# A fourth body for experts of at most 64 rows: the down projection with two products in place of three

## The reference

```
logits = h @ w_router + b_router                     # 256 x 8
top_logit, top_idx = top_k(logits, 2)
top_w = softmax(top_logit)
out_e = (silu(xb @ w1[e]) * (xb @ w3[e])) @ w2[e]    # w1, w3: 1024 x 3584, w2: 3584 x 1024
y = sum of top_w * out_e over the two experts of a token
```

## Time and profile before

| | us |
|---|---|
| median of 3 runs | 1878.74 (1877.62 to 1879.38) |
| the profiled execution | 1881.26 |
| its span, first to last instruction | 1879.6 |
| PE busy | 1727.6 (92%) |
| DVE busy | 1422.7 (76%) |
| ACT busy | 1042.6 (55%) |
| DMA | 502.62 MB, mean 267 GB/s |

### The profile page before, as it was taken

One profiled execution on the slowest core, in us unless ns is written; L12 is line 12 of the kernel. 1 busy time (PEld: TensorE's weight loads), 2 busy tenths in 40 slices (PEclk: granted clock), 3 DMA queues, 4 the chain that ended last, 5 costly groups with the idle time before them and its releaser, 6 DMA issues.

```text
span 1879.6 us, 22711 instructions
## 1 busy us (share of the span) xinstructions
PE 1727.6 (92%) x7882; PEld 1384.3 (74%) x7883; DVE 1422.7 (76%) x1201; ACT 1042.6 (55%) x817; POOL 25.6 (1%) x31
## 2 busy tenths in 40 slices
PE   1899979997999958999999989999999899999995
PEld 0687758886787736878878878888788787887884
DVE  7786877766686874897888875556589688888887
ACT  1464434433364424776767755545577676776773
POOL 0100000000100000000000000000000000000000
PEclk9898989999998977999999999999999999999998
DMA  9874458765474353998998975666599799899991
GB/s 359 308 278 157 157 179 302 280 224 180 170 284 156 112 202 113 361 364 311 366 340 304 378 277 178 211 231 210 192 371 370 256 372 365 301 368 335 340 368 66
DMA packets 210563, 502.62 MB, mean 267 GB/s; under 512 B 9137, under 2 KB 13409, under 8 KB 210481
## 3 DMA queue, kind: packets, MB, share of 16 engines
q1 hardware_dynamic: 208770, 496.15, 73.9%
q0 software_dynamic: 1712, 5.43, 0.9%
HBM read 500.50 MB, written 1.05 MB: 267 GB/s over the span
## 4 chain that ended last, share of the span: by engine, by line
PE 84%; DVE 8%; issue 5%; ACT 1%; DMA 1%; DVEq 0%; POOL 0%; ACTq 0%; SPq 0%; POOLq 0%
PE ps L1343 24%; PE ps L1344 23%; PE ps L1345 23%; PE ps L1349 2%; PE ps L1350 2%; PE ps L1737 2%; PE ps L1850 2%; DVE mod_acc L853 1%; PE ps L1778 1%; DVE stats L873 1%; PE ps L1467 1%; DVE w_lo L1224 1%; DVE w_lo L828 1%; DVE gates L1022 1%; DVE hbuf L890 1%
## 5 line engine op out<-in xcount | busy, mean ns | idle before, releaser
L1224 DVE TENSOR_TENSOR w_lo<-w_raw,w_hi 128x2048 fp32r<-128x2048 f32 x333 | 762.2, 2291 | 224.7 <-ACT w_hi L716 216.9
L716 ACT CAST w_hi<-w_raw 128x2048 fp32r<-128x2048 f32 x333 | 635.4, 1910 | 240.9 <-PE ps L1345 177.1
L1343 PE MATMUL ps<-w_hi,actT_hi 128*128 128x512 f32 (+1 forms) x1536 | 611.7, 398 | 22.6 <-issue 9.9
L1345 PE MATMUL ps<-w_hi,actT_lo 128*128 128x512 f32 (+1 forms) x1536 | 598.6, 390 | 0.0
L1344 PE MATMUL ps<-w_lo,actT_hi 128*128 128x512 f32 (+1 forms) x1536 | 598.0, 389 | 0.0
L1343 PEld LDWEIGHTS ps<-w_hi,actT_hi 128*128 128x128 f32 x1536 | 293.1, 191 | 89.6 <-issue 24.8
L1345 PEld LDWEIGHTS ps<-w_hi,actT_lo 128*128 128x128 f32 x1536 | 292.4, 190 | 60.9
L1344 PEld LDWEIGHTS ps<-w_lo,actT_hi 128*128 128x128 f32 x1536 | 293.1, 191 | 58.8 <-issue 2.3
L828 DVE TENSOR_TENSOR w_lo<-w_raw,w_hi 128x2048 fp32r<-128x2048 f32 x90 | 205.8, 2288 | 120.1 <-ACT w_hi L464 119.7
L464 ACT CAST w_hi<-w_raw 128x2048 fp32r<-128x2048 f32 x90 | 171.3, 1908 | 131.3 <-PE ps L1345 116.8
L1343 PE MATMUL ps<-w_hi,gT_hi 128*128 128x512 f32 x536 | 218.2, 407 | 16.9 <-DVE gT_lo L1247 13.1
(11 more groups left out here) (234 smaller groups left out, 1132.3 us busy)
## 6 DMA issues: line engine op xcount, KB each, us to landing
w_raw<-in_exp_w_dram SPq DMA_DIRECT2D x336, 1024.0 KB, 5.8
w_raw<-in_ffn_w_dram SPq DMA_DIRECT2D x33, 1024.0 KB, 5.2
w_raw<-in_w_mod_mix_dram SPq DMA_DIRECT2D x24, 1024.0 KB, 9.4
w_raw<-in_w_mod_ffn_dram SPq DMA_DIRECT2D x24, 1024.0 KB, 5.7
w_raw<-in_w_gate_dram SPq DMA_DIRECT2D x24, 1024.0 KB, 5.6
w_raw<-in_w_in_dram SPq DMA_DIRECT2D x14, 1024.0 KB, 7.5
w_raw<-in_w_out_dram SPq DMA_DIRECT2D x8, 1024.0 KB, 5.0
w_raw<-in_w_branch_c_dram SPq DMA_DIRECT2D x4, 1024.0 KB, 5.0
```

What stands on the lines that cost most here:

```text
L716: nc.scalar.copy(w_hi[:, i % SPLIT, :], w_raw[:, i % RING, :]).then_inc(split_hi, 1)
L1224: TTn(w_lo[:, i % SPLIT, :], w_raw[:, i % RING, :], w_hi[:, i % SPLIT, :].bitcast(F32), ALU.subtract).then_inc(piece_used, 1)
L1343: MM(to, hi, w_h, start=first, stop=False)
L1345: return MM(to, lo, w_h, start=False, stop=last)
```

## The change

A fourth body, `expert(1, few=True)`, takes experts of at most 64 rows. It packs high and low part for the down projection alone; the up projections stay as in `expert(1)`. Its `gT_hi` copy and its low part have 64 columns per 128 (128x256 in place of 128x512), the low part goes to columns 64 to 127 of the same tile, and `place` gets its second copy of 64 rows. `second_block` is gone from all three engines; the gather of a second block now stands at the start of the bodies for more than 128 rows, and one-block bodies only raise its semaphores.

```diff
ACT
-                    gathered_rows(0, 1)
-                    second_block(0, 1)
+                    gathered_rows(0, 1)
                     with nc.Fori(0, EXPERTS, ...) as e:
-                        def expert(blocks, packed=False):
+                        def expert(blocks, packed=False, few=False):
 gT_part:
-                                    n = HALF_P if b and packed else P
+                                    n = HALF_P if few or b and packed else P
 places:
-                                if packed:
+                                if packed or few:
+                                    half = blocks - 1
                                     ins.then_inc(place_copied, 1)
                                     act.wait_ge(place_copied, e + 1)
-                                    ins = A(place[HALF_P:P, 1, :], ps[0:HALF_P, 0, SEQ:2 * SEQ], ACT.Copy)
+                                    ins = A(place[HALF_P:P, half, :], ps[0:HALF_P, 0, half * SEQ:(half + 1) * SEQ], ACT.Copy)
 body's start:
+                            if blocks == 2:
+                                gathered_rows(1, e + 1)
+                            else:
+                                act.sem_inc(xg_hi_ready[1], 1)
 tail:
                                     gathered_rows(0, e + 2)
-                                    second_block(e + 1, e + 2)
DVE (its gathered_rows and second_block change in the same way)
 gT_part:
-                                for b in range(whole):
+                                for b in range(0 if few else whole):
                                     ins = TTn(gT_lo[:, b, :, :], ...)
-                                if packed:
-                                    ins = TTn(gT_hi[:, 1, :, HALF_P:P], ...)
+                                if packed or few:
+                                    half = blocks - 1
+                                    ins = TTn(gT_hi[:, half, :, HALF_P:P], ...)
PE
 body's start:
+                            pe.wait_ge(xg_hi_ready[0], e + 1)
+                            pe.wait_ge(xg_lo_ready[0], e + 1)
+                            if blocks == 2:
+                                gather(1, e + 1)
+                                pe.wait_ge(xg_hi_ready[1], e + 1)
+                                pe.wait_ge(xg_lo_ready[1], e + 1)
+                            else:
+                                pe.sem_inc(gathered_hi[1], 1)
+                                pe.sem_inc(gathered_lo[1], 1)
 down:
-                                            ins = multiply(b)(bank(2 * b + n), ...)
+                                            ins = (packed_product if few else multiply(b))(bank(2 * b + n), ...)
 end:
                                 gather(0, e + 2)
                                 scatter()
-                                second_block(e + 1, e + 2)
all three, at the choice of the body:
                         with pe.Else():
-                            expert(1)
+                            with pe.If(count > HALF_P):
+                                expert(1)
+                            with pe.Else():
+                                expert(1, few=True)
```

More of the change, by code:

```diff
@@ L814, in _ @@
                         with act.Else():
-                            expert(1)
+                            with act.If(count > HALF_P):
+                                expert(1)
+                            with act.Else():
+                                expert(1, few=True)
                     for t in range(TT):
@@ L1309, in tail @@
                                         TTn(part, part, bank(2 * t + c), ALU.add).then_inc(added, 1)
-                                if not last:
-                                    second_block(e + 1, e + 2)
                             with dve.If(e < EXPERTS - 1):
@@ L1323, in _ @@
                         with dve.Else():
-                            expert(1)
+                            with dve.If(count > HALF_P):
+                                expert(1)
+                            with dve.Else():
+                                expert(1, few=True)
                     dve.wait_ge(added, 4 * EXPERTS + 4)
@@ L1738, in gather, with expert @@
                             ins.then_inc(signal[b], 1)
-                    def second_block(e, n):
-                        with pe.If(pe.value_load(counts_i[0:1, bass.ds(e, 1)], min_val=0, max_val=SEQ) > P):
-                            pe.wait_ge(xg_hi_ready[0], n)
-                            pe.wait_ge(xg_lo_ready[0], n)
-                            gather(1, n)
-                        with pe.Else():
-                            pe.sem_inc(gathered_hi[1], 1)
-                            pe.sem_inc(gathered_lo[1], 1)
                     pe.wait_ge(pick_ready, 1)
                     gather(0, 1)
-                    second_block(0, 1)
                     with nc.Fori(0, EXPERTS, engines=[pe.engine], hint_back_edge=True) as e:
                         count = pe.value_load(counts_i[0:1, bass.ds(e, 1)], min_val=0, max_val=SEQ)
-                        def expert(blocks, packed=False):
+                        def expert(blocks, packed=False, few=False):
+                            pe.wait_ge(xg_hi_ready[0], e + 1)
+                            pe.wait_ge(xg_lo_ready[0], e + 1)
+                            if blocks == 2:
+                                gather(1, e + 1)
+                                pe.wait_ge(xg_hi_ready[1], e + 1)
+                                pe.wait_ge(xg_lo_ready[1], e + 1)
+                            else:
+                                pe.sem_inc(gathered_hi[1], 1)
+                                pe.sem_inc(gathered_lo[1], 1)
                             if packed:
                                 pe.wait_ge(packed_ready, e + 1)
-                            for b in range(blocks):
-                                pe.wait_ge(xg_hi_ready[b], e + 1)
-                                pe.wait_ge(xg_lo_ready[b], e + 1)
                             def turn_places():
@@ L1799, in down @@
                                         for n in range(2):
-                                            ins = multiply(b)(bank(2 * b + n), gT_hi[:, b, k, :], gT_lo[:, b, k, :], *split_piece(i, c, n * BANK, D),
+                                            ins = (packed_product if few else multiply(b))(bank(2 * b + n), gT_hi[:, b, k, :], gT_lo[:, b, k, :], *split_piece(i, c, n * BANK, D),
                                                               opens and k == 0, closes and k == 3)
```

20 lines of the change are left out of this document (6 added, 14 removed).

## The result

| | before | changed |
|---|---|---|
| median of 20 runs each, us | 1877.89 | 1883.26 |
| lowest and highest | 1873.93, 1883.11 | 1873.77, 1886.95 |
| the profiled execution | 1881.26 | 1884.75 |
| its span | 1879.6 | 1883.1 |
| PE instruction packets, 741 to 1900 us | 13 | 27 |

The ratio is 1.0028 with a 95% interval of 1.0019 to 1.0037: the changed kernel is slower by 5.4 us. The forecast was 1877.5, faster by a little; the time lies in its range and the sign is wrong. Not all of the 5.4 us lies where a profile can show it: in 7 of the 20 executions of the changed kernel the whole is 3.2 to 6.0 us longer than the span, in the other 13 it is 1.6 or 1.7 longer, as in all but two of the 53 executions of the kernel before that were run beside the experiments. The median span of the changed kernel is 1880.5; 1877.9 less 1.7 is 1876.2, so some 4.3 us are in the span (an estimate).

A forecast was written before the change was run, and what follows sets the result against it. PE was taken as the bound, with DVE close behind. Panels and ends were to gain 23.3 us and entries to cost 22.1, net -1.2: 1877.5 us for a median, range 1860 to 1892 (the forecast's own 1871 to 1884).

The forecast's parts named there:

- Part 1: Panels of five small experts: DVE's in-order queue becomes the bound, 16.34 us per panel, 0.71 us gained each, 3.55 per expert.
- The 404 GB/s of the forecast: Panel transfers: rate read for C pieces, used to put DMA at about 15.9 us per panel, just behind DVE.
- Rival (b): Panels: PE stays the bound because DVE is never late, about 1815 to 1830 us; chance 0.04.
- rival d: Panels: idle times of 0.2 and 0.9 us bring PE to 1.2 GHz, 39 us over 25 panels, 1916 us; chance 0.03.
- Part 2: Ends of five small experts: last matmuls start sooner, PE waits about 3.1 us, clock falls at each end; 5.6 us gained.
- Edits costed at nothing: Removed count test and value load, ACT's second place copy and handshake, longer ACT and DVE programs: no cost.
- Part 3: Entries of the eight experts: PE fetches code when another body has driven it out; cost 22.1 us, ends 5 and 40.
- The 3.2 for one more fetch: Expert entries: price of one more PE fetch in series, 3.2 us; it is expert 0's whole charge.
- The moved gather: Entry of packed expert 3: its second gather now stands behind the fetch it used to cover, +3.5 us.
- The picture behind it, that code stays until another body drives it out: Expert entries: code run lately stays resident, so entries pay after a switch of body, sometimes one expert later.
- rival (a): Expert entries: code stays resident or fetches hide under the scatter; Part 3 is 5 to 10 us, 1861 to 1866; chance 0.25.
- Rival (c): First matmul after each scatter: fetches in series, 3.2 us each, make it slower, 1895 us at 40 us cost; chance 0.18.

The follow-up runs named there:

- e5_order: e4_inner with DVE doing the next panel's A0 remainder before the gated product in the small body: 1852.5 us, ratio 0.9871.
- e4_inner: Changed kernel with one PE body for one-block experts, branching on the count around each pair of C pieces; ACT and DVE keep four bodies: 1856.8 us, ratio 0.9885.
- e3_never: Changed kernel with the small body taken only for a count of 0, so never; its code, branch and the moved gather stay: 1901.7 us, ratio 1.0122.
- e9_placed: Changed kernel with PE's plain and small bodies right behind the loop's head and the two large ones behind them; same work: 1867.9 us, ratio 0.9948.
- e10_unused_first: e3_never with the two one-block bodies swapped on all three engines, the unused one before the plain one: 1907.7 us, ratio 1.0165.
- e7_gather: Kernel before with only the second gather moved into the bodies for more than 128 rows; no small body: 1883.9 us, ratio 1.0032.
- e8_nobig: Changed kernel without the body for more than 192 rows, which no expert takes, on all three engines: 1871.1 us, ratio 0.9961.
- e6_tail: e5_order with DVE making gT_lo before the last C piece's remainder at the end of every one-block expert: 1845.5 us, ratio 0.9825.
- e1_twin: Changed kernel whose fourth body does the plain work, three matmuls per product and full copies: 1894.9 us, ratio 1.0092.

## Why the prediction was wrong

**Part 1, the panel: right.** The forecast was 16.34 us from turns to turns, 0.9 us idle before A0 and 0.2 before C1. The trace has 16.29, 0.84 (A0 starts 1.07 after C1's last matmul in place of 0.23; the profile lists 0.67 of it as idle) and 0.15 (C1's first matmul starts 0.38 after C0's last). The 25 panels of the small experts are 19.4 us shorter, against 17.8. The bound moved from PE to DVE's in-order queue, and e5_order shows it from the other side: reordering that queue alone took 0.25 us more off the panel. The transfers don't bind: no cast of ACT waits for a landing. (The 404 GB/s of the forecast stands in no slice of the earlier trace rows, which has 397 to 418 there; nothing rested on it.) Rival (b), PE stays the bound, is out, and so is the clock in the panels (rival d): the window of 1020 to 1037 us has a granted clock of 1.00 in spite of its idle time.

**Part 2, the ends: right in mechanism, a little low in size.** 2.95 us of wait against 3.1, and the clock fell in four of five ends (not in expert 7), against all five. From the last panel's turns to the scatter the five small experts gained 7.7 us, against 5.6. Parts 1 and 2 together gave 27.1 us where the forecast had 23.3.

**Edits costed at nothing: nearly right.** ACT's second place copy and its handshake appear in no wait of PE, and e4_inner, which keeps the four bodies of ACT and DVE, came out within a few us of what panels and ends give.

**Part 3, the entries: the step that failed.** Its sum was 22.1 us. The trace has 25.6 in the entries, and 5.8 more right behind them in the small experts, for which the sum had no term: after a wait of 3.4 to 7.3 us PE starts at the 1.2 GHz level. In the first 5 us after the entries of experts 0, 2, 4 and 5 the granted clock is 0.50, after that of expert 1 it is 0.66, after those of 6 and 7 it is 1.00. From expert 4's first product at 1354.13 fourteen of them take 6.06 us, which at 0.227 each would be 3.2. Over the five small experts the stretch from the first product to the first turns grew by these 5.8 us. So Part 3 should have read about 31 us in place of 22. The whole account of the span is -27.1 (panels and ends), +25.6 (entries), +5.8 (the first stretches), -1.5 (the bodies of experts 1, 3 and 6) and +0.8 (the stage starts later): +3.5 where -1.2 was forecast. By this sum, an estimate, it would be below zero without the slow first stretches, so a larger gain and a still larger cost were both missed, and the sign hung on a term that was left out.

Term by term in the entries: experts 0 to 2 were forecast +3.2, +4.8, +2.5 and came at +4.2, +5.2, +4.0. (The 4.8, taken from the difference of two whole periods, holds a slow stretch already: 1.3 us of it lie between the first product and the first turns of expert 5, where the granted clock is 0.66. The other prices don't. The 3.2 for one more fetch was taken from two first products that give 6.54 - 3.08 = 3.46.) The moved gather was forecast +3.5 and cost +0.7. Experts 4 and 5 were forecast +0.8 and 0, on the ground that the packed scatter covers the one and that the other pays today. They cost +7.2 and +4.0: 7.08 us of scatter cover does not help when PE stands another 7.25 us after it. Experts 6 and 7 were forecast +4.8 and +2.5 and cost +0.2 and 0. So the sum was near by terms that cancel, which is luck, as is the time's place within the range. The picture behind it, that code stays until another body drives it out, does not hold: expert 5 takes the body that expert 4 has just run and fetches again (six packets from its scatter on), expert 6 is the one plain body between two small ones in the second half and enters freely, and e3_never pays at experts 1 and 2 with no change of body at all. The place of a late entry, the first product, was read rightly, and its price was put too low: 2.5 to 4.8 us, where the five idle times are 3.4 to 7.3.

Fewer late entries would have made the change a gain: with one, as in e4_inner, it is 1.1% faster, still faster than the 1861 to 1866 that rival (a) gave for fetches that hide. Rival (c) named the mechanism and the point from which it decides, 2.9 us per entry; the mean is 25.6 / 8 = 3.2.

**What stays open.** Shown is that where the bodies stand in the program decides which entries are late (e9_placed, 15 us with the same work), and that code that never runs costs (18 us in e3_never and 24 in e10_unused_first against e7_gather, which lacks only the unused body and its branch; the removal of the largest body in e8_nobig -12). That the idle time is a fetch is shown by the packets. Which jumps need one is not: whether it is the distance of a jump, the amount of code that one round spans, or how bodies fall on packet borders is not told apart, since e8_nobig and e9_placed change all three. Of e3_never, e8_nobig and e10_unused_first it is not shown either that PE's copy of the unused body is what costs, for ACT and DVE have or lose theirs too; e9_placed, where PE's order alone changed, and e4_inner speak for PE. Also open is what spreads the runs of one kernel (e7_gather, 1873 to 1889).

## What to carry to other kernels

In a loop whose bodies are chosen by a branch, count the code of all bodies, also of those that are never taken. Here a variant that saves work inside a body paid when it shared the body's code and branched around the few instructions that differ, and lost as a body of its own. Then look at the first instruction of each round for idle time that the profile puts down to issue, and at the engine's instruction packets right before it, in every round and not in one; and look at the granted clock behind it, which here cost another 5.8 us. And before crediting PE with matmuls saved, lay out the other engines' in-order queues for one period: the gain here was 0.8 us per panel out of 1.9, and reordering DVE's queue brought another 11 us (e4_inner to e6_tail).

## What the runs showed of the hardware

- Unused code is dear. A body that no expert takes made the kernel 18 to 24 us slower, in a loop of eight rounds (e3_never and e10_unused_first against e7_gather).
- An idle time on issue at a round's first product is a fetch of PE's code, and its length goes with the packets. In the fourteen profiles, for experts 1, 2, 5, 6 and 7, one or two packets go with 2.9 to 4.6 us, four with 7.9 to 9.4; three go with 6.4 to 7.4 but for one case of 3.7.
- The late entries fall mostly in the first rounds and in those after the packed body (e8_nobig's expert 7 and e1_twin's expert 6 are exceptions). In both profiles of the changed kernel experts 6 and 7 enter at once though they alternate between bodies. The Trainium skill, "Runtime: NRT & Kernel Launch", section "Instruction fetch mechanics", has a taken branch to code outside the pages at hand stop for a fetch. The late entries agree with that, the free ones, into the same bodies, do not agree with its statement that only neighbouring pages are kept.
- An idle time of 2.95 us on PE was followed by the lower clock in four of five cases, one of 0.67 us, 25 times over, was not in the window looked at, and the 7.25 us at expert 4's entry were, as this window shows (length, busy of PE, PEld, DVE, ACT, POOL, then the granted clock 0.50, DMA share, GB/s):

```profile
1354.00:1360.00 6.00, 5.87 (x14) 4.62 (x15) 0.00 (x0) 0.35 (x1) 0.00 (x0) 0.50 0.02 5
```

- Some time is lost outside the span. In most executions the whole is 1.7 us longer than the span; in all six of e3_never it was 4.7 to 5.9, in those of e9_placed 3.4 to 5.1, in four of five of e10_unused_first 3.4 to 5.1 and in 7 of 20 of the changed kernel 3.2 to 6.0. No view shows what happens there.
